# Half of each modulation block's product sums moved from VectorE to GpSimd, as one product and ten folds

## The chip, the cores and the metric

The kernel runs on one core of a Trainium2 chip. The metric is the device time of one launch in microseconds (us), from runs that each give one time; three runs of the kernel before gave 2250.38, 2250.89 and 2251.74 us. The profile names the engines PE (TensorE; PEld is its weight load), DVE (VectorE), ACT (ScalarE), POOL (GpSimd) and SP (SyncE, which here only issues DMAs).

## The reference, cut to what matters

Two transformer-like models of width 1024 over 256 tokens, one behind the other, two layers each. Before every normalisation, and behind every residual branch, vectors of 1024 scale, shift or gate the activations. These vectors come from a conditioning vector and a wide matrix:

```
s_lat = silu(c); s_ctx = silu(c_ctx)
mod   = s_lat @ w_ada[l] + b_ada[l]          # l = 0, 1: 6 * 1024 columns
mod_c = s_ctx @ w_ada[l] + b_ada[l]
...
c_act = silu(c_2)
mod   = c_act @ mod_w[layer] + mod_b[layer]  # layer = 0, 1: 9 * 1024 columns
h     = rmsnorm(x, g) * (1 + scale) + shift
x     = x + gate * branch(h)
```

With one conditioning vector (or two, in the first layer) the matrix product is a sum of 1024 products for each column of the matrix: 30720 columns in all. The rest of the work, some thirty large matrix products (feed-forward, attention, convolution branches), runs on TensorE.

## The kernel before

**Slabs.** All large weights come in slabs: 128 partitions x up to 2048 floats, loaded by SP into `raw[:, p]` in two halves, where p is 0 or 1 in turn. ScalarE rounds each half into `w_hi` (L744), VectorE makes the remainder `w_lo` (L1333), and TensorE multiplies with three products (L2206 to L2208, or L2345 and L2350 where two of them are joined). A `Stage` is a run of such slabs; a body of its loop is two slabs, p = 0 and p = 1. Every engine walks the same list of stages and orders itself by semaphores. Each engine's instructions run in the order in which they are written: what VectorE waits for holds back all that is written behind it.

**Modulation blocks.** The modulation matrices are cut into 120 blocks of 256 columns, m = 0 to 119 (`N_MOD`); 48 belong to the first model, 72 to the second. Blocks 0 to 21 (`N_PE = 22`) are done on TensorE. From block 22 on a block lies transposed: for each of the 128 partitions two rows of 1024 weights, the halves c = 0 and c = 1. `modraw[:, c]` holds one such half of one block (512 KB), and `cact` holds the activated conditioning vectors, the same in every partition. One VectorE instruction (L1370) multiplies `modraw[:, c]` by `cact` and adds up the 1024 products into one column of `modcol`; an accumulator read of 0.08 us belongs to it. Blocks 22 to 31 (below `N_BOTH = 32`) need both conditioning vectors, and so a further product with the second one, into the scratch `mod_spare` (L1367).

**Where the blocks stand.** A stage's `mods` says how its blocks are spread. With `mods=1` a body does one block, half c = 0 at slab p = 0 and half c = 1 at slab p = 1 (the up stages of the feed-forward parts, and the down stages behind them). With `mods=2` each slab does a whole block. `mods` and `mod_product` (L1342, L1357) are called in the midst of a slab's other VectorE work.

**Loads.** GpSimd issues the loads (`load_mod`, L693). There is one buffer for each half. Half c of block m is loaded when VectorE has done half c of block m - 1: the wait is for `mod_done`, which L1370 raises by one for each half. VectorE waits for `mod_in[c]` before it reads. GpSimd does nothing else from block 22 on.

**Readers of the sums.** `mod_vector` (L1407) reads 8 columns of `modcol` behind a wait for `mod_done`, at the norms and at the ends of branches, on VectorE.

Of the kernel before, what the change touches and what calls it, by code (L numbers as in the profile page):

```python
# [26 lines left out]
D = 1024  # L27
# [40 lines left out]
N_MOD_A, N_MOD_B = 6 * D // 256, 9 * D // 256  # L68
N_MOD = 2 * N_MOD_A + 2 * N_MOD_B
# [3 lines left out]
N_PE = 22  # L73
N_BOTH = N_MOD_A + 8
# [5 lines left out]
LRU_WARM = (8, 3)  # L80
SBO_EARLY = 2
ST_AHEAD = 3

F32 = mybir.dt.float32
F32R = mybir.dt.float32r
ALU = mybir.AluOpType
# [7 lines left out]
AHEAD = N_FIRST + (N_TWO - N_FIRST) // 2 - 1  # L94
# [60 lines left out]
def build(nc, a):  # L155
# [93 lines left out]
    m = N_FIRST  # L249
# [87 lines left out]
    with ExitStack() as ctx:  # L337
        def sb(name, shape, dt=F32):
            return ctx.enter_context(nc.sbuf_tensor(name, shape, dt))

        def sem(name):
            return ctx.enter_context(nc.semaphore(name))
# [65 lines left out]
        mod_spare = view(3072, 2, D)  # L408
# [110 lines left out]
        first_in = [sem(f"first_in{k}") for k in range(N_FIRST)]  # L519
        mod_in = [sem("mod_in0"), sem("mod_in1")]  # L520
        mod_next_in = [sem("mod_next_in0"), sem("mod_next_in1")]
        mod_mm, mod_row, mod_turn, mod_done = (sem(f"mod_{k}") for k in ("mm", "row", "turn", "done"))
        vec_in = [sem(f"vec_in{k}") for k in range(2)]
        c_ready, masks_in, eps_set = sem("c_ready"), sem("masks_in"), sem("eps_set")
        dve_chain, act_chain = sem("dve_chain"), sem("act_chain")
# [162 lines left out]
        @block.gpsimd  # L688
        def _(pool):
            def load_mod(m, c, freed, used):  # L690

                pool.wait_ge(freed, used)
                nc.gpsimd.dma_start(modraw[:, c, :], a["w_mod"][m, :, D * c:D * (c + 1)]).then_inc(mod_in[c], 16)  # L693

            nc.gpsimd.memset(ccol[:], 0.0).then_inc(ccol_set, 1)
            for c in range(2):

                load_mod(N_FIRST, c, first_in[N_FIRST - 1], 16)
            nc.gpsimd.dma_start(res["x"][:], a["x"]).then_inc(setup_in[3], 16)
            nc.gpsimd.dma_start(cact[:].rearrange("p v d -> p (v d)"), a["vectors"][:, 0:2 * D]).then_inc(vec_in[1], 16)  # L700
            for m in range(N_FIRST + 1, N_TWO, 2):
                for c in range(2):

                    pool.wait_ge(mod_mm, 2 * N_FIRST if m == N_FIRST + 1 else 2 * m - 3 + c)
                    nc.gpsimd.dma_start(mod_next[:, c, :], a["w_mod"][m, :, D * c:D * (c + 1)])\
                        .then_inc(mod_next_in[c], 16)
                for c in range(2):
                    load_mod(m + 1, c, mod_mm, 2 * m - 1 + c)
            with pool.Fori(N_TWO + 1, N_PE) as m:
                for c in range(2):  # L710
                    load_mod(m, c, mod_mm, 2 * m - 1 + c)
            for c in range(2):

                load_mod(N_PE, c, mod_mm, 2 * N_PE - 1 + c)
            with pool.Fori(N_PE + 1, N_BOTH + 4) as m:
                for c in range(2):
                    load_mod(m, c, mod_done, 2 * m - 1 + c)

            pool.wait_ge(mod_done, 2 * N_BOTH)
            nc.gpsimd.dma_start(cact[:, 1, :], a["vectors"][:, 2 * D:3 * D]).then_inc(vec_in[1], 16)  # L720
            with pool.Fori(N_BOTH + 4, N_MOD) as m:
                for c in range(2):
                    load_mod(m, c, mod_done, 2 * m - 1 + c)


        @block.scalar
        def _(act):
# [202 lines left out]
            def st_terms(k):  # L930

                w, zm = sb_z[:, k % 3, 0], sb_z[:, k % 3, 1]
                act.wait_ge(st_zm, k + 1)
                wait_up(act, st_o, k - 2)
                link(nc.scalar.activation(w, zm, ACT.Abs))
                link(nc.scalar.activation(w, w, ACT.Exp, scale=-1.0))
                nc.scalar.activation(w, w, ACT.Ln, bias=1.0).then_inc(st_ln, 1)

            def st_weights(k):

                act.wait_ge(st_v, k + 1)
# [374 lines left out]
        def _(dve):  # L1316
# [25 lines left out]
            def mods(s, b, p, is_first=False, last=False):  # L1342

                if last_turn(s, b, p) is not None:
                    mod_sums(last_turn(s, b, p))
                if s.m0 < N_PE:
                    if s.mods == 2:
                        mod_sums(s.m0 + 2 * b + p - 1)
                    if s.mods == 1 and p == whole(s) and not (is_first and s.m0 in NOTHING_LEFT):
                        mod_sums(s.m0 + b - 1)  # L1350
                elif s.mods == 2:
                    for c in range(2):
                        mod_product(s, s.m0 + 2 * b + p, c)
                elif s.mods == 1 and not (is_first and s.mods_from):
                    mod_product(s, s.m0 + b - s.mods_from, p)

            def mod_product(s, m, p):  # L1357


                at = m if isinstance(m, int) else s.m0  # L1360
                second_block = at >= 2 * N_MOD_A
                dve.wait_ge(c_ready, 4 if second_block else 3)
                dve.wait_ge(mod_in[p], 16 * (m - AHEAD))
                if at < N_BOTH:

                    dve.wait_ge(mod_done, 2 * m - 1 + p)
                    nc.vector.scalar_tensor_tensor(out=mod_spare[:, p, :], in0=modraw[:, p, :], scalar=1.0, in1=cact[:, 1, :],  # L1367
                                                   op0=ALU.mult, op1=ALU.mult,
                                                   accum_out=modcol[:, 1, bass.ds(2 * m + p, 1)])
                nc.vector.scalar_tensor_tensor(out=modraw[:, p, :], in0=modraw[:, p, :], scalar=1.0,  # L1370
                                               in1=cact[:, int(second_block), :], op0=ALU.mult, op1=ALU.mult,
                                               accum_out=modcol[:, 0, bass.ds(2 * m + p, 1)]).then_inc(mod_done, 1)

            def pad_edges(s):

# [31 lines left out]
            def mod_vector(r, v, out, plus, ks=range(DC), need=None):  # L1407

                if r["kind"] == "a":
                    base, bcol, w = 48 * r["l"], f"b_ada{r['l']}", 1 if r["x"] == "ctx" else 0  # L1410
                else:
                    base, bcol, w = 96 + 72 * r["l"], f"mod_b{r['l']}", 0
                k, n = ks.start, len(ks)
                dve.wait_ge(mod_done, 2 * (r["need"] if need is None else need))
                src = modcol[:, w, base + 8 * v + k:base + 8 * v + k + n]
                link(nc.vector.scalar_tensor_tensor(out=cols[:, out, k:k + n], in0=src, scalar=plus,
                                                    in1=pcol(bcol, 8 * v + k, n), op0=ALU.add, op1=ALU.add))
# [675 lines left out]
            def do_stick(n):  # L2093
                sv = next(s for what, s in plan if what == "slabs" and s.kind == "v" and s.arg["heads"] == SB_H)
                for i in range(ST_AHEAD, SB_P + 3):
                    if ST_AHEAD < i <= SB_P:
                        st_softplus(i - 1)
# [101 lines left out]
        def _(pe):  # L2199
# [850 lines left out]
```

## Time and profile before

| | |
|---|---|
| median of three runs | 2250.89 us |
| the profiled execution's own time | 2255.51 us |
| its span on the core, first to last instruction | 2253.5 us |
| PE busy | 2167.5 us (96%) |
| DVE busy | 1808.6 us (80%) |
| ACT busy | 1246.7 us (55%) |
| POOL busy | 120.4 us (5%) |
| mean granted TensorE clock | 0.986 |

The profile counts an engine as busy while an instruction runs on it; starts and durations come from one execution. Between two instructions of one engine that follow closely, the records overlap a little (a 1024-element VectorE instruction reads 1.22 us, and the next starts 1.14 us after it), so distances from start to start are the better measure in a full stretch. Idle time is put down to what ended it ("the releaser").

### The profile page before, as it was taken

What the parts mean: (1) busy time and instruction counts of PE and PEld (TensorE: products, weight loads), DVE (VectorE), ACT (ScalarE), POOL (GpSimd) and SP (SyncE); (2) the same over time, 40 slices, a digit from 0 to 9 for tenths busy, and PEclk for the clock granted to TensorE, in tenths of its full rate; (3) what the DMA queues carried; (4) which work ended last, traced back from release to release, by engine and by line L of the source; (5) the groups of instructions that cost most, each with busy time, mean ns of one, the idle gap of its engine ahead of it and who ended that gap; (6) DMA issues with size and microseconds to landing.
All of it is one profiled execution on the core that took longest, in us unless ns stands there. A gap on an engine that the chain in (4) does not pass through costs nothing.

```text
span 2253.5 us, 42557 instructions
## 1 busy us (share of the span) xinstructions
PE 2167.5 (96%) x15168; PEld 1984.7 (88%) x15168; DVE 1808.6 (80%) x3102; ACT 1246.7 (55%) x1981; POOL 120.4 (5%) x232
## 2 busy tenths in 40 slices
PE   7998999999999989999999999999999999999998
PEld 5897988888788779889999889997989989999898
DVE  4886797777677768978998988877988888889865
ACT  4466457544223333576664664656664655686653
POOL 0100000000010100000000001000010001000000
PEclk8999999999999999999999999999999999999999
DMA  9845553434475555535788688773788788636754
GB/s 360 284 132 172 182 175 127 151 130 133 137 261 184 180 178 172 178 118 166 239 271 275 227 282 266 231 245 122 246 277 272 230 280 279 232 125 192 243 177 132
DMA packets 139741, 465.59 MB, mean 207 GB/s; under 512 B 16208, under 2 KB 20432, under 8 KB 138064
## 3 DMA queue, kind: packets, MB, share of 16 engines
q1 hardware_dynamic: 102560, 339.41, 44.8%
q0 software_dynamic: 32688, 120.08, 17.1%
q10 hardware_dynamic: 4352, 4.20, 0.6%
q8 instruction: 92, 1.51, 0.3%
q14 instruction: 49, 0.40, 0.0%
HBM read 462.57 MB, written 1.05 MB: 206 GB/s over the span
## 4 chain that ended last, share of the span: by engine, by line
PE 74%; DVE 12%; ACT 6%; issue 4%; DMA 3%; ACTq 0%; SPq 0%; DVEq 0%; POOL 0%; POOLq 0%
PE bank_pair L2206 16%; PE bank_pair L2208 16%; PE bank_pair L2207 16%; PE bank_pair L2345 12%; PE bank_pair L2350 6%; DVE w_lo L1333 3%; DMA modraw<-in_w_mod 2%; DVE arena L1648 2%; ACT w_hi L744 2%; PE bank_pair L2335 2%; DVE small L1762 1%; PE ps_o L2219 1%; ACT arena L1011 1%; DVE arena L1823 1%; PE ps_o L2853 1%
## 5 line engine op out<-in xcount | busy, mean ns | idle before, releaser
L1333 DVE TENSOR_TENSOR w_lo<-raw,w_hi 128x1024 fp32r<-128x1024 f32 (+2 forms) x672 | 735.5, 1118 | 124.8 <-ACT w_hi L744 120.3
L744 ACT ACTIVATE w_hi<-raw 128x1024 fp32r<-128x1024 f32 (+2 forms) x672 | 640.5, 969 | 334.2 <-PE bank_pair L2208 193.1
L2206 PE MATMUL bank_pair<-e_both,w_hi 128*128 128x256 f32 (+1 forms) x1632 | 470.9, 289 | 11.3 <-DVE w_lo L1333 7.7
L2206 PE MATMUL bank_pair<-h_joint,w_hi 128*128 128x256 f32 (+1 forms) x1488 | 464.5, 312 | 8.1 <-DVE w_lo L1333 3.4
L2207 PE MATMUL bank_pair<-e_both,w_hi 128*128 128x256 f32 (+1 forms) x1632 | 464.1, 284 | 0.0
L2208 PE MATMUL bank_pair<-e_both,w_lo 128*128 128x256 f32 (+1 forms) x1632 | 464.0, 284 | 0.0
L2207 PE MATMUL bank_pair<-h_joint,w_hi 128*128 128x256 f32 (+1 forms) x1488 | 456.7, 307 | 0.0
L2208 PE MATMUL bank_pair<-h_joint,w_lo 128*128 128x256 f32 (+1 forms) x1488 | 456.5, 307 | 0.0
L2206 PEld LDWEIGHTS bank_pair<-e_both,w_hi 128*128 128x128 f32 x1632 | 314.9, 193 | 22.0 <-DVE w_lo L1333 9.9
L2207 PEld LDWEIGHTS bank_pair<-e_both,w_hi 128*128 128x128 f32 x1632 | 315.2, 193 | 0.3
L2208 PEld LDWEIGHTS bank_pair<-e_both,w_lo 128*128 128x128 f32 x1632 | 315.0, 193 | 0.0
L2206 PEld LDWEIGHTS bank_pair<-h_joint,w_hi 128*128 128x128 f32 x1488 | 285.4, 192 | 33.2 <-issue 14.1
L2345 PE MATMUL bank_pair<-h_joint,w_hi 128*128 128x512 f32 x1216 | 304.6, 393 | 0.1
L2207 PEld LDWEIGHTS bank_pair<-h_joint,w_hi 128*128 128x128 f32 x1488 | 285.7, 192 | 12.9
L2208 PEld LDWEIGHTS bank_pair<-h_joint,w_lo 128*128 128x128 f32 x1488 | 285.5, 192 | 12.4
L1370 DVE SCALAR_TENSOR_TENSOR modraw<-modraw,cact 128x1024 f32<-128x1024 f32 x196 | 238.1, 1220 | 32.5 <-DMA modraw<-in_w_mod 32.2
L2345 PEld LDWEIGHTS bank_pair<-h_joint,w_hi 128*128 128x128 f32 x1216 | 218.8, 189 | 39.2 <-DVE e_plain L1473 0.3
L693 POOL DMA_DIRECT2D modraw<-in_w_mod x216 | 114.1, 529 | 1954.2 <-DVE modraw L1370 1742.0
L2350 PEld LDWEIGHTS bank_pair<-h_joint,w_lo 128*128 128x128 f32 x1216 | 165.9, 191 | 11.8
L2350 PE MATMUL bank_pair<-h_joint,w_lo 128*128 128x256 f32 x1216 | 169.6, 283 | 0.0
L1648 DVE SCALAR_TENSOR_TENSOR arena<-arena,par 128x256 f32<-128x256 f32 x360 | 149.8, 479 | 4.0 <-PE bank_pair L2807 3.8
L2032 DVE SCALAR_TENSOR_TENSOR arena<-bank_pair,par,arena 128x510 f32<-128x510 f32 (+1 forms) x168 | 93.0, 621 | 47.8 <-ACT arena L1174 47.6
(258 smaller groups left out, 2636.1 us busy)
## 6 DMA issues: line engine op xcount, KB each, us to landing
modraw<-in_w_mod POOLq DMA_DIRECT2D x216, 512.0 KB, 5.2
raw<-in_w_gu SPq DMA_DIRECT2D x176, 512.0 KB, 5.5
raw<-in_w_up SPq DMA_DIRECT2D x88, 512.0 KB, 5.4
raw<-in_w_gate SPq DMA_DIRECT2D x48, 512.0 KB, 4.1
raw<-in_w_dn SPq DMA_DIRECT2D x64, 384.0 KB, 4.8
raw<-in_w_dn SPq DMA_DIRECT2D x64, 320.0 KB, 4.0
raw<-in_w_glu SPq DMA_DIRECT2D x24, 512.0 KB, 5.4
raw<-in_w_merge SPq DMA_DIRECT2D x24, 512.0 KB, 3.7
```

Source lines behind the costliest of these rows:

```text
L693: nc.gpsimd.dma_start(modraw[:, c, :], a["w_mod"][m, :, D * c:D * (c + 1)]).then_inc(mod_in[c], 16)
L744: nc.scalar.activation(w_hi[:, p, HALF * f:HALF * f + w], raw[:, p, HALF * f:HALF * f + w], ACT.Copy)\
L1333: nc.vector.tensor_tensor(w_lo[:, p, at], raw[:, p, HALF * f:HALF * f + w], w_hi[:, p, at].bitcast(F32), ALU.subtract).then_inc(lo_ready, 1)
L1370: nc.vector.scalar_tensor_tensor(out=modraw[:, p, :], in0=modraw[:, p, :], scalar=1.0, in1=cact[:, int(second_block), :], op0=ALU.mult, op ...
L1648: ins = nc.vector.scalar_tensor_tensor(out=o, in0=u, scalar=w[:, j, t:t + 1], in1=o, op0=ALU.mult, op1=ALU.add)
L2032: nc.vector.scalar_tensor_tensor(out=o, in0=i_, scalar=taps[:, c, 0:1] if left else taps[:, c, 2:3], in1=o, op0=ALU.mult, op1=ALU.add)\
L2206: nc.tensor.matmul(out, l[0], r[0], start=start, stop=False)
L2207: nc.tensor.matmul(out, l[0], r[1], start=False, stop=False)
L2208: return nc.tensor.matmul(out, l[1], r[0], start=False, stop=stop)
L2335: ins = nc.tensor.matmul(pb[p][:, f, 0:T], raw[:, p, c:c + P], h_plain[:, k, :], start=k == 0, stop=k == DC - 1)
L2345: nc.tensor.matmul(pb[p][:, f, :].rearrange("p (e t) -> p e t", e=2), w_hi[:, p, c:c + P], h_sides[:, :, k, :], start=k == 0, stop=False)
L2350: ins = nc.tensor.matmul(pb[p][:, f, T:2 * T], w_lo[:, p, c:c + P], h_hi[:, k, :], start=False, stop=k == DC - 1)
```

## The change

GpSimd takes the half c = 1 of every block from 22 on. It multiplies `modraw[:, 1]` by the vector (1024 elements) and then folds: it adds the upper half of the row to the lower half, 512 elements, then 256, and so on down to 2, and a last add of one element writes the column of `modcol`. That is 11 instructions for each product sum, each but the first behind a wait for the one ahead (`mod_step`). Blocks 22 to 31 have two product sums. The last add raises `mod_pool`.

VectorE keeps half c = 0, at p = 0 of a `mods=1` body and once per slab with `mods=2`; its instruction raises `mod_done` by two. GpSimd's queue holds the loads too: half 1 of the next block is issued behind its own last add, and half 0 behind that, once VectorE has done half 0 of the block (`next_block`). `mod_vector` waits for `mod_pool` as well.

```diff
+            def product_sum(tile, v, out, done):
+                nc.gpsimd.tensor_tensor(tile, modraw[:, 1, :], cact[:, v, :], ALU.mult).then_inc(mod_step, 1)
+                for k in range(1, FOLDS):
+                    w = D >> k
+                    pool.wait_ge(mod_step, done + k)
+                    nc.gpsimd.tensor_tensor(tile[:, 0:w], tile[:, 0:w], tile[:, w:2 * w], ALU.add).then_inc(mod_step, 1)
+                pool.wait_ge(mod_step, done + FOLDS)
+                return nc.gpsimd.tensor_tensor(out, tile[:, 0:1], tile[:, 1:2], ALU.add)
...
+            def first_vector(m, v):
+                pool.wait_ge(mod_in[1], 16 * (m - AHEAD))
+                product_sum(modraw[:, 1, :], v, modcol[:, 0, bass.ds(2 * m + 1, 1)], FOLDS * (m + N_BOTH - 2 * N_PE))                    .then_inc(mod_pool, 1)
+            def next_block(m):
+                load_mod(m, 1, mod_pool, m - N_PE)
+                load_mod(m, 0, mod_done, 2 * m)
...
-                    for c in range(2):
-                        mod_product(s, s.m0 + 2 * b + p, c)
-                elif s.mods == 1 and not (is_first and s.mods_from):
-                    mod_product(s, s.m0 + b - s.mods_from, p)
+                    mod_product(s, s.m0 + 2 * b + p)
+                elif s.mods == 1 and p == 0 and not (is_first and s.mods_from):
+                    mod_product(s, s.m0 + b - s.mods_from)
...
-                dve.wait_ge(mod_done, 2 * (r["need"] if need is None else need))
+                blocks = r["need"] if need is None else need
+                dve.wait_ge(mod_done, 2 * blocks)
+                if blocks > N_PE:
+                    dve.wait_ge(mod_pool, blocks - N_PE)
```

GpSimd, the loop over blocks with one vector: before.

```order
L693 ISA [waits mod_done]
L693 DMA modraw<-in_w_mod 128x1024
L693 ISA [waits mod_done]
L693 DMA modraw<-in_w_mod 128x1024
L721 REGISTER_ALU
L721 COMPARE_AND_BRANCH
```

The same loop after the change, down to the third fold; seven more instructions of the same kind follow, ending in one element.

```order
L694 ISA [waits mod_pool]
L694 DMA modraw<-in_w_mod 128x1024
L693 REGISTER_ALU
L694 REGISTER_ALU [waits mod_done]
L694 DMA modraw<-in_w_mod 128x1024
L734 ISA
L718 TENSOR_TENSOR modraw<-modraw,cact 128x1024 [waits mod_in1]
L721 ISA
L722 TENSOR_TENSOR modraw<-modraw 128x512 [waits mod_step]
L721 REGISTER_ALU
L722 TENSOR_TENSOR modraw<-modraw 128x256 [waits mod_step]
L721 REGISTER_ALU
```

The two loads stood in the queue alone; the product and the folds now stand between one pair of loads and the next.

VectorE, from the middle of an up body of the second model's feed-forward (L1333 makes the low part of a half slab, L2053, L2066 and L2075 belong to the gated activation): before.

```order
L1333 TENSOR_TENSOR w_lo<-raw,w_hi 128x1024 [waits hi_ready]
L2053 ISA [waits upb_hi]
L2053 TENSOR_TENSOR e_both<-arena,e_both 128x256
L2066 TENSOR_TENSOR arena<-bank_pair,arena 128x512 [waits upb_side]
L1370 ISA [waits mod_in1,c_ready]
L1370 SCALAR_TENSOR_TENSOR modraw,modcol<-modraw,cact 128x1024
L2069 REGISTER_ALU
L2075 TENSOR_TENSOR arena<-arena 128x256 [waits upb_silu]
```

The same place after the change (L1369, L2091, L2104 and L2113 are the same lines of the new file).

```order
L1369 TENSOR_TENSOR w_lo<-raw,w_hi 128x1024 [waits hi_ready]
L2091 ISA [waits upb_hi]
L2091 TENSOR_TENSOR e_both<-arena,e_both 128x256
L2104 TENSOR_TENSOR arena<-bank_pair,arena 128x512 [waits upb_side]
L2107 REGISTER_ALU
L2113 TENSOR_TENSOR arena<-arena 128x256 [waits upb_silu]
```

The product at p = 1 and its wait for the load are gone; the one at p = 0, with its wait for `mod_in0`, stands where it stood.

## Rows read from the trace of the kernel before

**Rows 1.** The page: busy time and share of the span by engine.
```profile
PE 2167.5 (96%) x15168; PEld 1984.7 (88%) x15168; DVE 1808.6 (80%) x3102; ACT 1246.7 (55%) x1981; POOL 120.4 (5%) x232
```
**Rows 2.** Stretches with blocks: length, busy us (instructions) by engine, clock, DMA share, GB/s.
```profile
core 0: us, PE busy (x) PEld busy (x) DVE busy (x) ACT busy (x) POOL busy (x), PEclk, DMA share, GB/s
520.00:570.00 50.00, 50.00 (x222) 41.41 (x221) 38.09 (x55) 20.40 (x29) 2.64 (x5) 1.00 0.43 140
620.00:650.00 30.00, 30.00 (x134) 24.87 (x133) 21.83 (x36) 6.58 (x7) 4.23 (x8) 1.00 0.72 246
1085.00:1186.00 101.00, 101.00 (x844) 101.00 (x843) 101.00 (x181) 64.36 (x106) 9.52 (x18) 1.00 0.82 271
1310.00:1383.00 73.00, 73.00 (x432) 64.78 (x431) 62.05 (x93) 42.44 (x66) 7.39 (x14) 1.00 0.84 274
1386.00:1419.00 33.00, 33.00 (x277) 33.00 (x277) 30.50 (x50) 11.48 (x16) 4.22 (x8) 1.00 0.89 290
```
**Rows 3.** Waits of PE, whole span: for whom, us in total, times, longest.
```profile
PE bank_pair L2206 <- DVE w_lo L1333: 14.0, 12, 2.7
PE bank_pair L2206 <- DVE arena L2032: 11.9, 3, 4.9
```
**Rows 4.** Groups by line and form: count, busy us, mean ns, idle before and its releaser.
```profile
L1333 DVE TENSOR_TENSOR w_lo<-raw,w_hi 128x1024 fp32r<-128x1024 f32 x464 | 555.3, 1222 | 94.6 <-ACT w_hi L744 92.4
L1370 DVE SCALAR_TENSOR_TENSOR modraw<-modraw,cact 128x1024 f32<-128x1024 f32 x196 | 238.1, 1220 | 32.5 <-DMA modraw<-in_w_mod 32.2
L1367 DVE SCALAR_TENSOR_TENSOR arena<-modraw,cact 128x1024 f32<-128x1024 f32 x20 | 24.4, 1220 | 4.2 <-issue 4.2
```
**Rows 5.** The load line L693 on GpSimd: durations, and time from issue to landing.
```profile
L693 POOL DMA_DIRECT2D modraw<-in_w_mod x216: 527/527/662, 33.0 to 2105.4; - x108
DMA to landing us min/median/max: 3.7/5.2/9.9
```
**Rows 6.** GpSimd in an up stretch: start us, us, what, idle before and its releaser.
```profile
1315.26 0.53 POOL L693 DMA_DIRECT2D modraw<-in_w_mod  x1 [4.00 <-DVE modraw L1370]
1320.84 0.53 POOL L693 DMA_DIRECT2D modraw<-in_w_mod  x1 [5.05 <-DVE modraw L1370]
1326.42 0.53 POOL L693 DMA_DIRECT2D modraw<-in_w_mod  x1 [5.05 <-DVE modraw L1370]
```
**Rows 7.** GpSimd in down stretches, and (668.95) behind a body with both halves together.
```profile
617.86 0.53 POOL L693 DMA_DIRECT2D modraw<-in_w_mod  x1 [4.29 <-DVE modraw L1370]
626.37 0.53 POOL L693 DMA_DIRECT2D modraw<-in_w_mod  x1 [4.29 <-DVE modraw L1370]
668.95 0.53 POOL L693 DMA_DIRECT2D modraw<-in_w_mod  x1 [0.61 <-DVE modraw L1370]
1389.12 0.53 POOL L693 DMA_DIRECT2D modraw<-in_w_mod  x1 [6.31 <-DVE modraw L1370]
1396.97 0.53 POOL L693 DMA_DIRECT2D modraw<-in_w_mod  x1 [3.54 <-DVE modraw L1370]
```
**Rows 8.** GpSimd's only computing instructions: start us, us, what.
```profile
0.49 0.10 POOL L3043 MEMSET const-uint8-127<- 128x1 uint8 x1
0.88 0.31 POOL L695 MEMSET ccol<- 128x256 f32 x1 [0.29 <-POOLq L3043]
```
**Rows 9.** VectorE in one slab of an up stretch, in order of time.
```profile
1313.38 1.22 DVE L1370 SCALAR_TENSOR_TENSOR modraw<-modraw,cact 128x1024 f32<-128x1024 f32 x1
1315.02 2.36 DVE L1333 TENSOR_TENSOR w_lo<-raw,w_hi 128x1024 fp32r<-128x1024 f32 x2
1318.36 0.69 DVE L2066 TENSOR_TENSOR arena<-bank_pair,arena 128x512 f32<-128x512 f32 x1 [0.65 <-ACT arena L1211]
```
**Rows 10.** Stretches of 4 us about a pause of TensorE (columns as in rows 2).
```profile
578.00:582.00 4.00, 0.55 (x3) 0.13 (x1) 1.93 (x3) 1.96 (x3) 0.00 (x0) 0.84 0.69 278
582.00:586.00 4.00, 2.51 (x6) 2.06 (x7) 4.00 (x8) 0.63 (x1) 0.00 (x0) 0.50 0.00 0
586.00:590.00 4.00, 4.00 (x16) 3.19 (x15) 2.18 (x5) 1.56 (x3) 0.53 (x1) 0.81 0.38 132
```

More of the change, by code:

```diff
@@ L82 @@
 ST_AHEAD = 3
+FOLDS = 10
 F32 = mybir.dt.float32
@@ L521, in build @@
         mod_next_in = [sem("mod_next_in0"), sem("mod_next_in1")]
-        mod_mm, mod_row, mod_turn, mod_done = (sem(f"mod_{k}") for k in ("mm", "row", "turn", "done"))
+        mod_mm, mod_row, mod_turn, mod_done, mod_pool, mod_step = (sem(f"mod_{k}") for k in ("mm", "row", "turn", "done", "pool", "step"))
         vec_in = [sem(f"vec_in{k}") for k in range(2)]
@@ L714, in _ @@
                 load_mod(N_PE, c, mod_mm, 2 * N_PE - 1 + c)
-            with pool.Fori(N_PE + 1, N_BOTH + 4) as m:
-                for c in range(2):
-                    load_mod(m, c, mod_done, 2 * m - 1 + c)
-            pool.wait_ge(mod_done, 2 * N_BOTH)
-            nc.gpsimd.dma_start(cact[:, 1, :], a["vectors"][:, 2 * D:3 * D]).then_inc(vec_in[1], 16)
-            with pool.Fori(N_BOTH + 4, N_MOD) as m:
-                for c in range(2):
-                    load_mod(m, c, mod_done, 2 * m - 1 + c)
+            def product_sum(tile, v, out, done):
[6 more added lines that the diff above has]
+                return nc.gpsimd.tensor_tensor(out, tile[:, 0:1], tile[:, 1:2], ALU.add)
@@ new lines, in both_vectors @@
+            def both_vectors(m):
+                pool.wait_ge(mod_in[1], 16 * (m - AHEAD))
+                product_sum(mod_spare[:, 1, :], 1, modcol[:, 1, bass.ds(2 * m + 1, 1)], 2 * FOLDS * (m - N_PE))
+                product_sum(modraw[:, 1, :], 0, modcol[:, 0, bass.ds(2 * m + 1, 1)], 2 * FOLDS * (m - N_PE) + FOLDS)                    .then_inc(mod_pool, 1)
+            def first_vector(m, v):
+                pool.wait_ge(mod_in[1], 16 * (m - AHEAD))
+                product_sum(modraw[:, 1, :], v, modcol[:, 0, bass.ds(2 * m + 1, 1)], FOLDS * (m + N_BOTH - 2 * N_PE))                    .then_inc(mod_pool, 1)
@@ new lines, in next_block @@
+            def next_block(m):
+                load_mod(m, 1, mod_pool, m - N_PE)
+                load_mod(m, 0, mod_done, 2 * m)
+            pool.wait_ge(c_ready, 3)
+            pool.wait_ge(mod_done, 2 * N_PE + 2)
+            both_vectors(N_PE)
+            with pool.Fori(N_PE + 1, N_BOTH) as m:
+                next_block(m)
+                both_vectors(m)
+            next_block(N_BOTH)
+            nc.gpsimd.dma_start(cact[:, 1, :], a["vectors"][:, 2 * D:3 * D]).then_inc(vec_in[1], 16)
@@ L726, in _ @@
+            first_vector(N_BOTH, 0)
+            with pool.Fori(N_BOTH + 1, 2 * N_MOD_A) as m:
+                next_block(m)
+                first_vector(m, 0)
+            next_block(2 * N_MOD_A)
+            pool.wait_ge(c_ready, 4)
+            first_vector(2 * N_MOD_A, 1)
+            with pool.Fori(2 * N_MOD_A + 1, N_MOD) as m:
+                next_block(m)
+                first_vector(m, 1)
         @block.scalar
@@ L1351, in mods, with mod_product @@
                 elif s.mods == 2:
-                    for c in range(2):
-                        mod_product(s, s.m0 + 2 * b + p, c)
-                elif s.mods == 1 and not (is_first and s.mods_from):
-                    mod_product(s, s.m0 + b - s.mods_from, p)
-            def mod_product(s, m, p):
+                    mod_product(s, s.m0 + 2 * b + p)
+                elif s.mods == 1 and p == 0 and not (is_first and s.mods_from):
+                    mod_product(s, s.m0 + b - s.mods_from)
+            def mod_product(s, m):
                 at = m if isinstance(m, int) else s.m0
@@ L1362, in mod_product @@
                 dve.wait_ge(c_ready, 4 if second_block else 3)
-                dve.wait_ge(mod_in[p], 16 * (m - AHEAD))
+                dve.wait_ge(mod_in[0], 16 * (m - AHEAD))
                 if at < N_BOTH:
-                    dve.wait_ge(mod_done, 2 * m - 1 + p)
-                    nc.vector.scalar_tensor_tensor(out=mod_spare[:, p, :], in0=modraw[:, p, :], scalar=1.0, in1=cact[:, 1, :],
+                    dve.wait_ge(mod_done, 2 * m)
+                    nc.vector.scalar_tensor_tensor(out=mod_spare[:, 0, :], in0=modraw[:, 0, :], scalar=1.0, in1=cact[:, 1, :],
                                                    op0=ALU.mult, op1=ALU.mult,
-                                                   accum_out=modcol[:, 1, bass.ds(2 * m + p, 1)])
-                nc.vector.scalar_tensor_tensor(out=modraw[:, p, :], in0=modraw[:, p, :], scalar=1.0,
+                                                   accum_out=modcol[:, 1, bass.ds(2 * m, 1)])
+                nc.vector.scalar_tensor_tensor(out=modraw[:, 0, :], in0=modraw[:, 0, :], scalar=1.0,
                                                in1=cact[:, int(second_block), :], op0=ALU.mult, op1=ALU.mult,
-                                               accum_out=modcol[:, 0, bass.ds(2 * m + p, 1)]).then_inc(mod_done, 1)
+                                               accum_out=modcol[:, 0, bass.ds(2 * m, 1)]).then_inc(mod_done, 2)
             def pad_edges(s):
```

## The prediction

> **What bounds the kernel now.** I read the page first. TensorE is busy 96% of the span, VectorE 80%, GpSimd 5% [rows 1]. The reader is to see that the engine that gets lighter is not the one that sets the time. The view by stretches then shows where blocks are worked: in all five TensorE is busy from end to end at full clock, while VectorE is at 73 to 100% and GpSimd at 5 to 14% [rows 2]. In the waits of TensorE the largest for VectorE are 14.0 and 11.9 us over the whole span [rows 3]; that is what a lighter VectorE can give back, at most some 20 us of 2253.5. Third I read GpSimd's own queue, since the change fills it. In an up stretch a load is issued every 5.58 us, two to a block, so a block takes 11.16 us [rows 6]; in down stretches 7.85 to 8.5 us [rows 7]. GpSimd sleeps between loads because VectorE has not freed the buffer, and the load lands 5.2 us after its issue [rows 5]. Each block so carries one landing in a period set by TensorE, with VectorE's product beside it.
>
> **What goes from VectorE.** Blocks 22 to 119 are 98; each loses one L1370, and the ten blocks 22 to 31 one L1367 as well: 108 instructions of 1.22 us [rows 4], 132 us, and with 0.08 us for each accumulator read 140 us. In the up stretch 13 instructions in 73 us leave 7; VectorE falls from 62.05 to about 54 us of 73 [rows 2]. As TensorE has no idle time in these stretches, I cost this gain at nothing. It is worth at most about 20 us, by rows 3. The stretch 1085 to 1186, where VectorE too is busy throughout [rows 2], gains no time either, since TensorE is full there as well.
>
> **What GpSimd gets.** 108 product sums of 11 instructions. The trace has no two-input instruction on GpSimd, so a sum's length C is bounded. It handles 1024 elements in the product and 1023 in the folds, 2047 in all. The fast end is VectorE's pace: 1.14 us from start to start for 1024 elements (two together last 2.36, one alone 1.22 [rows 4, 9]), 1.11 ns each, 2.3 us. The slow end takes GpSimd's own row: 256 elements written in 0.31 us against 0.10 for one [rows 8], 0.82 ns each; two reads and a write one after the other are 2.5 ns, 5.0 us. I take 4.2 us, nearer to GpSimd's row because it is the same engine. Then there is the fixed part, 11 times: between 0.10 us (the shortest instruction [rows 8]) and 0.61 us (GpSimd woken by a semaphore, with its register work, until the next load starts [rows 7]). I take 0.25, since the folds wait for GpSimd itself and carry one register operation: 2.75 us. Undisturbed, C is 7.0 us, between 3.4 and 11.7.
>
> Last comes what VectorE and GpSimd do to each other. No row shows them computing at once. The lower bound is zero; the upper is each of 11 steps standing behind one `w_lo` of 1.14 us, 12.5 us. VectorE would be busy half the time in a stretched block, its instructions are 0.4 to 1.2 us long, so I take 0.2 us a step, 2 us. **C = 9 us.**
>
> The Trainium skill has prices for both. GPSIMD Engine Reference, section 3.1, gives 4497 ns for an add of 2048 elements against VectorE's 2293; an estimate from it is 4.5 us for the 2047 elements, and C without disturbance would be 7.3, the sum below about 170 us; no row here shows a GpSimd add.
>
> **What waits for it.** This is the step that carries the forecast. GpSimd's queue now reads: load half 1 of block m, load half 0 of block m, product and folds of block m. Half 1 can only be loaded when its buffer has been folded, and half 0 is issued behind that. So the shortest period of a block is one landing plus one sum: 5.2 + C = 14.2 us. VectorE waits for half 0 in the midst of a body; behind the wait stand that body's gated activation and the next slab's `w_lo`, then TensorE. A period over the spacing of before is thus lost in full, block after block.
>
> From the issue times of L693 I took the spacing of all blocks. Of those from 32 on, 55 stand in up-like places at 11.0 us in the mean (for instance rows 6) and 23 in down stretches at 8.0 (rows 7; 8 issues, 4 blocks, in 33 us [rows 2]). Eight follow a pause of over 30 us.
> - Up: 55 x (14.2 - 11.0) = 176 us.
> - Down: 23 x (14.2 - 8.0) = 143 us.
> - Two vectors, period 5.2 + 18 = 23.2 us: blocks 23 to 27 come every 21.7 us (one slab takes about 10.8: 50 us hold five loads [rows 2]), 5 x 1.5 = 8 us; four of blocks 28 to 31 every 7.9 us, 4 x 15.3 = 61 us.
> - At each of the eight pauses GpSimd gets ahead by a load and a sum. Stepping through the 97 blocks (VectorE's time is the later of its old spacing and the last sum's end + 0.53 + 5.2 + 1.3; a sum ends C after its load has landed) gives 321 us for the whole, so the pauses give back about 67.
>
> The same stepping gives 12 us at C = 3.4, 34 at 5, 51 at 5.6, 145 at 7, 413 at 10, 597 at 12 and 781 at 14. Below about 5 it is nearly free, above 6 each further us costs some 70 to 90.
>
> **Edits at nothing.** The first sums follow VectorE's first product, block 22, with 17 us to the next: hidden. The new wait in `mod_vector` asks for blocks that lie eight or more back at the norms; it would cost up to one C at the few ends of branches if it did not. The load of the third vector, once, is 0.53 us. The two loads cost 0.53 us each [rows 5], which the queue held before too. TensorE's pauses can lower its clock: after a pause of some 5 us the granted clock is 0.50, the 1.2 GHz level, and about 6 us later it is rising again [rows 10]. In a down block TensorE would pause 6 us and then run some us at half pace, 8 us of work becoming about 11. The period of 14.2 hides this; with C below 7 it would show, at up to 3 us x 23.
>
> **The sum.** 2255.5 (the profiled execution) + 321 = 2576 us. The median of the three runs is 4.6 us below that execution, so the forecast is 2572 us.
>
> **Rivals.**
>
> A. *GpSimd runs undisturbed.* C = 7 and the period 12.2. Up 55 x 1.2, down 23 x 4.2, two vectors 40, pauses less: 145 us, 2396 us. For it speaks that the two engines work on different rows of memory; nothing shows against it.
>
> B. *The two engines shut each other out.* Each fold that finds VectorE reading waits for its end, and VectorE's `w_lo` waits for the 1024-element product. After a landing both start at once, GpSimd's 11 steps and VectorE's backlog of about 8 instructions, so nearly each step waits some 0.5 us: C = 7 + 5.5 = 12.5, about +640 us, 2890 us. For it: VectorE is at 85 to 92% in the down and up stretches [rows 2]. Against it: no row. The Trainium skill has this as a rule (SBUF — State Buffer, Who interferes with whom): a VectorE instruction with two SBUF inputs and a GpSimd instruction that reads SBUF exclude each other for the whole instruction. `w_lo` and L1370 are of that kind. No run so far shows it.
>
> C. *Short folds.* If small instructions cost about 0.1 us and elements about VectorE's pace to half as slow again, C is 3.5 to 5 and the period 8.7 to 10.2: up stretches stay whole, down stretches lose 1 to 2 us a block. That is +12 to +34 us, about 2275.
>
> D. *Faster.* The same C below 4, and VectorE's 140 us shorten the stretches that follow it: the waits of rows 3 shrink by half and the waits of VectorE for modulation loads, 32.5 us [rows 4], in part. That gives up to -15 us, 2236. It decides at C = 4, where the period, 9.2 us, exceeds the down spacing by little. Against it speaks GpSimd's 0.61 us to wake: at that price the fixed part alone is 6.7 us.
>
> **How the numbers follow.** The forecast, C from 7.5 to 11.5, has 0.42. A has 0.22, B 0.15, C 0.11, D with the cases near zero 0.10. Slower by over 0.2% (4.5 us, about what a measurement can tell from no change): 0.42 + 0.22 + 0.15 + 0.08 of C, 0.87; within 0.2%: 0.05; faster: 0.08. The range runs from 2280 (C about 4.5 to 5) to 2840 (C = 12): it leaves out D and part of C below, about 0.12, and most of B's upper part, about 0.08.
>
> **What the profile of after would show.** The load of half 1 issued right behind the last one-element add, and a distance from one such load to the next of 14 us in up and down stretches alike, where 11.2 and 8 stood. VectorE's largest new wait would be its product's, for the load of half 0. TensorE busy would fall to about 75 to 80% in rows like rows 2, with clock below 1.00 in down stretches. A GpSimd sum is read from start to start: 9 us. In rival A it is 7 with `w_lo` still at 1.22 us; in B `w_lo` has a longer mean and the folds' starts fall on the ends of VectorE's instructions; in C and D the up stretches keep 11.2 us. The forecast is wrong if GpSimd still idles before its loads in the up stretches, waiting for VectorE.

## The result, and the profile after

The changed kernel takes 2773.4 us (median of four runs, 2766.5 to 2775.4) against 2250.6 us before: 1.231 times as long, 95% interval 1.230 to 1.233. The profiled execution took 2766.5 us, its span is 2764.8 us. So the change costs 523 us (511 between the two profiled executions), where the prediction had 321. The measured time lies in its range (2280 to 2840), near the upper end.

The page of the changed kernel, its part on busy time and its chain of work that ended last (its first line answers [rows 1]); below it the same chain in the kernel before.

```profile
PE 2323.9 (84%) x15168; PEld 2093.9 (76%) x15168; DVE 1932.1 (70%) x2886; ACT 1241.2 (45%) x1981; POOL 1123.5 (41%) x1420
...
POOL 32%; PE 22%; issue 20%; DVE 15%; ACT 5%; DMA 4%; POOLq 2%; DVEq 0%; ACTq 0%; SPq 0%
```
```profile
PE 74%; DVE 12%; ACT 6%; issue 4%; DMA 3%; ACTq 0%; SPq 0%; DVEq 0%; POOL 0%; POOLq 0%
```

TensorE fell from 96 to 84% of the span. VectorE has 216 records fewer (108 products and their accumulator reads), yet its busy time rose, from 1808.6 to 1932.1 us: it lost 140 us of work and took on some 260 us by which its other instructions got longer. GpSimd, which was 5% busy and 0% of the chain, now heads the chain with 32%. VectorE's `w_lo` of 1024 elements, at 1222 ns before [rows 4]:

```profile
L1369 DVE TENSOR_TENSOR w_lo<-raw,w_hi 128x1024 fp32r<-128x1024 f32 x464 | 626.5, 1374 | 118.2 <-ACT w_hi L780 117.7
```

GpSimd's queue in an up stretch, in order of time (start us, us, what, idle before and its releaser); this answers [rows 6].

```profile
1606.20 1.19 POOL L694 DMA_DIRECT2D modraw<-in_w_mod  x2 [0.66 <-POOL modcol L724]
1610.50 2.40 POOL L718 TENSOR_TENSOR modraw<-modraw,cact 128x1024 f32<-128x1024 f32 x1 [3.11 <-DMA modraw<-in_w_mod]
1612.97 7.22 POOL L722 TENSOR_TENSOR modraw<-modraw 128x512 f32<-128x512 f32 x9
1620.37 0.19 POOL L724 TENSOR_TENSOR modcol<-modraw 128x1 f32 x1 [0.18 <-POOL modraw L722]
1621.38 1.20 POOL L694 DMA_DIRECT2D modraw<-in_w_mod  x2 [0.82 <-POOL modcol L724]
```

This is the cycle of the prediction. The one-element add ends at 1620.56; 0.82 us later both loads of the next block are issued. From load to load it is 15.18 us, where 11.16 us stood before. A sum, from the start of its product to the end of its last add, takes 10.06 us here; over all 108 sums the mean is 10.1, over those of blocks with one vector 10.2. Over the 80 distances between blocks with one vector that hold no pause the mean is 16.3 us, up and down stretches alike; the ten with two vectors are 24.1 us apart.

Who waits in the changed kernel: waits of VectorE, then of TensorE (us in total, times, longest); the second answers [rows 3].

```profile
DVE modraw L1405 <- DMA modraw<-in_w_mod: 412.8, 70, 15.3
...
PE bank_pair L2244 <- DVE w_lo L1369: 221.9, 61, 11.8
PE bank_pair L2388 <- DVE w_lo L1369: 54.6, 20, 5.6
```

VectorE's product (now L1405) waits 412.8 us for the load of half 0; it was 32.5 us [rows 4]. That load stands behind the sum in GpSimd's queue, so the releaser that the row names is the DMA, and the cause stands one step behind it. TensorE waits behind VectorE for `w_lo`.

Three stretches with blocks, columns as in [rows 2]: an up, a down and a last down stretch.

```profile
1595.00:1687.00 92.00, 72.88 (x380) 61.55 (x379) 61.70 (x76) 36.16 (x58) 61.96 (x78) 0.91 0.55 189
1687.00:1753.00 66.00, 47.65 (x333) 46.64 (x333) 42.29 (x56) 16.76 (x25) 43.68 (x52) 0.85 0.55 174
2098.00:2160.00 62.00, 43.21 (x281) 42.39 (x280) 32.91 (x39) 13.48 (x19) 43.22 (x52) 0.81 0.52 167
```

TensorE is busy 70 to 79% of them, and the granted clock fell to 0.81 to 0.91 from 1.00. No engine is full. That is what a loop of waits looks like: a landing, a sum, and an issue, one behind the other.

### The profile page after: what moved, and what is told of

Its sections match the earlier page's. It is cut to its first block, busy times and chain, and to the rows that moved or that the text cites. A ratio compares the mean times of both kernels' runs of the same rounds, so it can differ in the third digit from the quotient of the medians.

```text
span 2764.8 us, 44709 instructions
## 1 busy us (share of the span) xinstructions
PE 2323.9 (84%) x15168; PEld 2093.9 (76%) x15168; DVE 1932.1 (70%) x2886; ACT 1241.2 (45%) x1981; POOL 1123.5 (41%) x1420
## 4 chain that ended last, share of the span: by engine, by line
POOL 32%; PE 22%; issue 20%; DVE 15%; ACT 5%; DMA 4%; POOLq 2%; DVEq 0%; ACTq 0%; SPq 0%
POOL modraw L722 19%; POOL modraw L718 7%; PE bank_pair L2244 5%; PE bank_pair L2245 5%; PE bank_pair L2246 5%; DVE w_lo L1369 4%; POOL arena L722 3%; DVE arena L1686 2%; DMA modraw<-in_w_mod 2%; POOL modraw L694 2%; ACT w_hi L780 2%; PE bank_pair L2383 2%; POOLq L721 1%; POOL arena L718 1%; PE bank_pair L2388 1%
## 5 line engine op out<-in xcount | busy, mean ns | idle before, releaser
L1369 DVE TENSOR_TENSOR w_lo<-raw,w_hi 128x1024 fp32r<-128x1024 f32 (+2 forms) x672 | 852.0, 1291 | 139.9 <-ACT w_hi L780 138.2
L722 POOL TENSOR_TENSOR modraw<-modraw 128x512 f32<-128x512 f32 (+8 forms) x882 | 628.6, 713 | 69.1
L2244 PE MATMUL bank_pair<-e_both,w_hi 128*128 128x256 f32 (+1 forms) x1632 | 493.2, 302 | 103.2 <-DVE w_lo L1369 97.6
L2244 PE MATMUL bank_pair<-h_joint,w_hi 128*128 128x256 f32 (+1 forms) x1488 | 478.7, 322 | 79.5 <-DVE w_lo L1369 71.9
L2245 PE MATMUL bank_pair<-e_both,w_hi 128*128 128x256 f32 (+1 forms) x1632 | 482.0, 295 | 0.0
L2245 PE MATMUL bank_pair<-h_joint,w_hi 128*128 128x256 f32 (+1 forms) x1488 | 466.4, 313 | 0.0
L1405 DVE SCALAR_TENSOR_TENSOR modraw<-modraw,cact 128x1024 f32<-128x1024 f32 x98 | 174.9, 1785 | 413.1 <-DMA modraw<-in_w_mod 412.8
L2244 PEld LDWEIGHTS bank_pair<-e_both,w_hi 128*128 128x128 f32 x1632 | 334.2, 205 | 119.2 <-DVE w_lo L1369 104.3
L2244 PEld LDWEIGHTS bank_pair<-h_joint,w_hi 128*128 128x128 f32 x1488 | 293.2, 197 | 113.3 <-DVE w_lo L1369 80.2
L718 POOL TENSOR_TENSOR modraw<-modraw,cact 128x1024 f32<-128x1024 f32 x98 | 237.9, 2427 | 314.8 <-DMA modraw<-in_w_mod 314.6
L2383 PE MATMUL bank_pair<-h_joint,w_hi 128*128 128x512 f32 x1216 | 331.7, 418 | 20.8 <-DVE arena L2104 20.8
L2245 PEld LDWEIGHTS bank_pair<-e_both,w_hi 128*128 128x128 f32 x1632 | 334.6, 205 | 0.5
L2246 PEld LDWEIGHTS bank_pair<-e_both,w_lo 128*128 128x128 f32 x1632 | 333.6, 204 | 0.0
L2245 PEld LDWEIGHTS bank_pair<-h_joint,w_hi 128*128 128x128 f32 x1488 | 294.3, 198 | 13.9
L2383 PEld LDWEIGHTS bank_pair<-h_joint,w_hi 128*128 128x128 f32 x1216 | 235.3, 203 | 70.8 <-issue 23.0
```

What stands on the lines that cost most here:

```text
L718: nc.gpsimd.tensor_tensor(tile, modraw[:, 1, :], cact[:, v, :], ALU.mult).then_inc(mod_step, 1)
L722: nc.gpsimd.tensor_tensor(tile[:, 0:w], tile[:, 0:w], tile[:, w:2 * w], ALU.add).then_inc(mod_step, 1)
L1369: nc.vector.tensor_tensor(w_lo[:, p, at], raw[:, p, HALF * f:HALF * f + w], w_hi[:, p, at].bitcast(F32), ALU.subtract).then_inc(lo_ready, 1)
L1405: nc.vector.scalar_tensor_tensor(out=modraw[:, 0, :], in0=modraw[:, 0, :], scalar=1.0, in1=cact[:, int(second_block), :], op0=ALU.mult, op ...
L2244: nc.tensor.matmul(out, l[0], r[0], start=start, stop=False)
L2245: nc.tensor.matmul(out, l[0], r[1], start=False, stop=False)
```

## The experiments

Each experiment ran beside the kernel before on the same chip, which gave 2251.1 us; that is the "before" of this section. Two theories stood against each other. *Queue*: the loss is the order, a period of one landing and one sum, with VectorE's load standing behind the sum. *Port*: the loss is that reads by GpSimd and reads by VectorE exclude each other.

### What taking the products off VectorE is worth: e4_no_half1

```diff
-                nc.gpsimd.tensor_tensor(tile, modraw[:, 1, :], cact[:, v, :], ALU.mult).then_inc(mod_step, 1)
-                for k in range(1, FOLDS):
...
-                return nc.gpsimd.tensor_tensor(out, tile[:, 0:1], tile[:, 1:2], ALU.add)
+                return nc.gpsimd.tensor_tensor(out, modraw[:, 1, 0:1], modraw[:, 1, 1:2], ALU.add)
```

> The sums of the halves c = 1 are left out on all engines but for one add of one element on GpSimd; the loads stay. It gives what taking 108 products (140 us of its time) off VectorE is worth if nothing is paid for it. Theory 'TensorE sets the time before': 0 to 20 us under before, 2230 to 2250 us. Rival 'VectorE was the bound in stretches such as 1085 to 1186 us, where it is busy throughout': 30 us or more under before.

Measured: 2247.1 us, ratio 0.998 (0.9975 to 0.9994): 4 us under before. The gain that the change aims at was never there. VectorE's 140 us were covered by TensorE, also in the stretch where VectorE was busy throughout. About the same stretch in this kernel, columns as in [rows 2]:

```profile
1080.00:1180.00 100.00, 100.00 (x836) 100.00 (x835) 91.35 (x162) 64.67 (x106) 19.09 (x26) 1.00 0.79 277
```

VectorE has 8.65 us of idle time in 100 us; TensorE is as full as before. The rival, that VectorE set the time there, would have given 30 us or more, and falls.

One thing about the kernels that follow: in e1, e6, e7 and e10 GpSimd's loop over blocks is written out, while the changed kernel, e2, e3, e4 and e8 keep it. From the last add of a sum to the issue of the next load it is 0.76 us (mean of 79) in the changed kernel, with register work and a branch between, and 0.31 us in e1 and e6.

### Writes in the place of reads: e1_writes_only

```diff
+W0 = 1024
...
-                nc.gpsimd.tensor_tensor(tile, modraw[:, 1, :], cact[:, v, :], ALU.mult).then_inc(mod_step, 1)
-                for k in range(1, FOLDS):
...
-                    nc.gpsimd.tensor_tensor(tile[:, 0:w], tile[:, 0:w], tile[:, w:2 * w], ALU.add).then_inc(mod_step, 1)
+                for k in range(FOLDS):
...
+                    nc.gpsimd.memset(tile[:, 0:W0], 0.0).then_inc(mod_step, 1)
```

> The product and the ten folds on GpSimd are replaced by ten instructions that only write (1024 elements each, 0.82 ns per element by the memset row, about 0.94 us each), each still behind a wait for the one ahead, then the last add; so the length of a sum stays about 10 us but GpSimd reads almost nothing. The sums of the halves c = 1 are left out. The loop over blocks is written out. Theory 'queue' (period = landing + sum, VectorE waits for the load that stands behind the sum in GpSimd's queue): period stays 15 to 16 us, time 2650 to 2770 us, though w_lo is back at 1.22 us. Theory 'port' (the time is lost because reads of GpSimd and VectorE exclude each other): time falls to 2250 to 2320 us.

Measured: 2737.2 us (ratio 1.217, 1.214 to 1.219). Its groups by form (count, busy us, mean ns, idle before and its releaser), as in [rows 4]:

```profile
L1369 DVE TENSOR_TENSOR w_lo<-raw,w_hi 128x1024 fp32r<-128x1024 f32 x464 | 554.4, 1219 | 117.0 <-ACT w_hi L780 116.4
L1405 DVE SCALAR_TENSOR_TENSOR modraw<-modraw,cact 128x1024 f32<-128x1024 f32 x98 | 119.9, 1224 | 553.8 <-DMA modraw<-in_w_mod 553.5
...
L722 POOL MEMSET modraw<- 128x1024 f32 x980 | 934.1, 953 | 383.0 <-DMA modraw<-in_w_mod 332.3
```

`w_lo` is at 1219 ns, as before [rows 4], and the time is still 486 us over before. So the queue alone, with sums of this length, makes a loss of this size; VectorE need not be slowed at all. But the sum's length is a free quantity here, since I set it near that of the changed kernel (10.5 us in the mean, against 10.2). What makes the changed kernel's sum that long is the next question.

### The length of an undisturbed sum: e6_writes_7us

The shortest records of the eleven instructions in the changed kernel (512 elements, for example, range from 1278 to 2272 ns in a sample of 36) are 2332, 1278, 733, 453, 317, 250, 219, 202, 202, 193 and 192 ns: 6.4 us, and with ten gaps of about 0.09 us 7.3 us. The shortest of the changed kernel's 108 sums, as a whole, is 7.31 us, so this length does occur. This kernel, an edit of e1, was to write for that long; its sums have a mean of 7.0 us.

```diff
-W0 = 1024
+W0 = 606
```

> As e1_writes_only, with 606 instead of 1024 elements in each of the ten writing instructions, so that a sum lasts 7.3 us, the sum of the shortest durations of the changed kernel's eleven instructions. It stands for the change on a chip where GpSimd's reads disturb nobody. The sums of the halves c = 1 are left out. Theory 'queue, and collisions of reads lengthen the sum': by the stepping with C = 7.3, 171 us over before, 2405 to 2440 us; the rest of the 522 us, some 340, then belongs to reads. Rival 'a sum's own length makes the whole loss': it would have to stay above 2650 us.

Measured: 2463.1 us (ratio 1.094, 1.092 to 1.096), 212 us over before; the stepping had 171, and the time lies above the range that was expected. From its queue, in order of time:

```profile
1412.61 6.59 POOL L722 MEMSET modraw<- 128x606 f32 x10 [4.78 <-DMA modraw<-in_w_mod]
1419.28 1.09 POOL L724 TENSOR_TENSOR modcol<-modraw 128x1 f32<-128x1 f32 x1
1420.67 1.10 POOL L695 DMA_DIRECT2D modraw<-in_w_mod  x2 [0.30 <-POOL modcol L724]
1427.32 6.59 POOL L722 MEMSET modraw<- 128x606 f32 x10 [5.56 <-DMA modraw<-in_w_mod]
```

From the issue at 1420.67 to the next start it is 6.65 us; the mean over 79 blocks with one vector is 5.75 us, and from the end of one sum to the start of the next 6.1 us, where the stepping has 5.2 (with 5.9 it gives 225). So the longer way from sum to sum can account for the missing 41 us.

The comparison splits the loss: 212 us are there without the reads, the other 310 only with them. Nearly all of the 310 lies in the distance between blocks, 13.2 us in the mean here and 16.3 in the changed kernel, and that is the sum's length, 7.0 against 10.2; the way from sum to sum is about equal (6.1 and 5.9 us), since e6's quicker issue and its longer landing cancel. One small share of the 310 is not the reads' own: e6's sums are 0.3 us shorter than an undisturbed one, worth some 20 us by the 78 us for each us of sum between e6 and e1 (274 us for 3.5 us). So the reads are worth rather 290 us.

### The order of the queue: e2_two_buffers

```diff
+        mod_more = sb("mod_more", [P, D])
...
-                load_mod(m, 1, mod_pool, m - N_PE)
-                load_mod(m, 0, mod_done, 2 * m)
...
+            def one(k, odd, work, *v):
+                load1(k + odd, 1 - odd)
+                work(k, odd, *v)
+                next0(k + odd, 1 - odd)
```

Odd blocks have their half 1 in `mod_more`. `load1` loads half 1 of the next block into the other buffer, `work` is the block's product and folds, and `next0` loads half 0 of the next block.

> Half 1 gets a second buffer; its next load is issued ahead of the sum instead of behind it. Same sums, same order of folds. Theory 'queue': the period becomes one sum and two issues, about 11.5 us; up stretches (11.2 us before) lose next to nothing, down stretches 3.5 us a block, the two-vector blocks in the down stretch some 50 us together: 2350 to 2420 us. Theory 'port': as many reads collide in less time, so the time stays near 2770, at least above 2650 us.

Measured: 2489.5 us (ratio 1.107, 1.105 to 1.109). The queue's order is worth 284 us, which *port* alone cannot explain. But the time is 70 us above the range that I had given to *queue*, so the order is not all. Its period in a down stretch:

```profile
1411.57 3.05 POOL L720 TENSOR_TENSOR mod_more<-mod_more,cact 128x1024 f32<-128x1024 f32 x1
1414.70 7.50 POOL L724 TENSOR_TENSOR mod_more<-mod_more 128x512 f32<-128x512 f32 x9
...
1424.63 2.41 POOL L720 TENSOR_TENSOR modraw<-modraw,cact 128x1024 f32<-128x1024 f32 x1
```

From product to product it is 13.06 us: a sum of 11.8 us and two issues, and no waiting for a landing. (Over all blocks with one vector the mean distance is 12.8 us.) In the stretch from 1500 to 1560 us (columns as in [rows 2]) both engines that share the reads are nearly full, and TensorE is not:

```profile
1500.00:1560.00 60.00, 51.46 (x338) 47.74 (x339) 54.60 (x63) 25.64 (x39) 52.31 (x62) 0.94 0.67 215
```

### Two buffers and no reads: e7_two_buffers_writes

The edit is that of e6_writes_7us, made in e2_two_buffers, and GpSimd's loop is written out.

> e2_two_buffers with the writing instructions of e6_writes_7us in the place of the sums (7.3 us, the sums of the halves c = 1 left out). The stepping with two buffers and C = 7.3 gives 36 us over before: 2275 to 2300 us. If e2's 239 us came from its queue order or from load traffic and not from reads, it would stay near 2450 us or more.

Measured: 2270.3 us (ratio 1.008, 1.006 to 1.011), 19 us over before; the stepping had 36, and the range began at 2275. The landing hidden and the reads gone, nearly the whole loss is gone. Of e2's 239 us, 219 go with the reads and the loop. The loop's part is small but not separated: between sums e2 takes 1.20 or 1.70 us by turns, the branch in every second one, where e7 takes 1.03 at the shortest; 0.4 us for each of 80 to 90 distances would be some 35 us.

### One instruction that reads, or two that write: e3_product_only, e10_short_writes

```diff
-FOLDS = 10
+FOLDS = 1
...
                 nc.gpsimd.tensor_tensor(tile, modraw[:, 1, :], cact[:, v, :], ALU.mult).then_inc(mod_step, 1)
-                for k in range(1, FOLDS):
-                    w = D >> k
-                    pool.wait_ge(mod_step, done + k)
-                    nc.gpsimd.tensor_tensor(tile[:, 0:w], tile[:, 0:w], tile[:, w:2 * w], ALU.add).then_inc(mod_step, 1)
```

> The folds are left out (the sums of the halves c = 1 are left out): GpSimd makes the product of 1024 elements and the last add of one, a sum of about 2.9 us. Theory 'queue': by the stepping of the prediction 5 to 15 us over before, 2255 to 2270 us. Theory 'port': GpSimd's reading time falls from 9.2 to 2.7 us a sum, so about 0.29 of the 522 us remain: about 2400 us.

```diff
-FOLDS = 10
+FOLDS = 2
+W0 = 1024
...
-                nc.gpsimd.tensor_tensor(tile, modraw[:, 1, :], cact[:, v, :], ALU.mult).then_inc(mod_step, 1)
...
+                for k in range(FOLDS):
...
+                    nc.gpsimd.memset(tile[:, 0:W0], 0.0).then_inc(mod_step, 1)
```

> As e3_product_only, with two writing instructions of 1024 elements (0.95 us each) in the place of the product: a sum of about 2.4 us that reads next to nothing. The sums of the halves c = 1 are left out. Theory 'e3's 52 us are collisions of reads': the time is that of e4_no_half1, 2245 to 2255 us. Rival 'they come from the loads being issued behind the product': it stays at 2285 to 2305 us.

Measured: 2303.0 us for the product alone (ratio 1.022, 1.020 to 1.025) and 2246.2 us with writes (0.998, 0.997 to 0.999). With a sum this short the queue costs nothing, looped or written out, so e10 sits beside e4, and the 57 us between e3 and e10 go with the reads: 0.53 us for each of 108 products. `w_lo` of 1024 elements has a mean of 1467 ns in e3 and 1220 ns in e10; the first row is of e3_product_only, the second of e10_short_writes.

```profile
L1365 DVE TENSOR_TENSOR w_lo<-raw,w_hi 128x1024 fp32r<-128x1024 f32 x464 | 669.6, 1467 | 113.1 <-ACT w_hi L776 112.4
```
```profile
L1369 DVE TENSOR_TENSOR w_lo<-raw,w_hi 128x1024 fp32r<-128x1024 f32 x464 | 555.2, 1220 | 118.2 <-ACT w_hi L780 117.7
```

Both theories missed e3: *queue* had 15 us at most, since its stepping has no term for a slower VectorE, and *port*, scaled by reading time, had about 150.

### The blocks with two vectors: e8_one_sum_each

```diff
-                product_sum(mod_spare[:, 1, :], 1, modcol[:, 1, bass.ds(2 * m + 1, 1)], 2 * FOLDS * (m - N_PE))
+                nc.gpsimd.tensor_tensor(modcol[:, 1, bass.ds(2 * m + 1, 1)], cact[:, 0, 0:1], cact[:, 1, 0:1], ALU.mult)
```

> The changed kernel without GpSimd's sum for the second vector in blocks 22 to 31 (that sum is left out). The stepping with C = 10.2 gives 431 us with two sums and 352 with one: 79 us less, so about 2695 us. If two sums in a block were hidden, since six of the ten blocks stand 21 us apart, it would be within 30 us of the changed kernel.

Measured: 2707.1 us (ratio 1.203, 1.198 to 1.207), 66 us under the changed kernel, against 79 expected. The edit also lowers the counts that the waits for `mod_step` ask for. The second sum of these ten blocks is not hidden.

### What the runs add up to

| | reads as in the change | writes only |
|---|---|---|
| load behind the sum | 2773.4 (+523) | 2463.1 (+212), sum of 7.0 us |
| load ahead of the sum | 2489.5 (+239) | 2270.3 (+19), sum of 7.1 us |
| product only | 2303.0 (+52) | 2246.2 (-5) |

The columns differ by 310, 219 and 57 us; of the first some 20 are the shorter sum, of the second a part is the loop, and the rest goes with the reads. The two causes strengthen each other, since 212 and 239 are 451 and the change costs 523: a collision makes the sum longer, and the queue charges each longer sum to every block. None of these kernels is faster than the kernel before by more than 5 us, and e4, which leaves the work out, puts what VectorE's relief is worth at 4.

## How the reads collide

The timeline of VectorE and GpSimd in the changed kernel over 4.6 us, from narrow windows (start us, us, what):

```profile
1612.50 1.48 DVE L1405 SCALAR_TENSOR_TENSOR modraw<-modraw,cact 128x1024 f32<-128x1024 f32 x1 [3.07 <-DMA modraw<-in_w_mod]
1612.97 2.16 POOL L722 TENSOR_TENSOR modraw<-modraw 128x512 f32<-128x512 f32 x1
...
1613.91 1.50 DVE L2113 TENSOR_TENSOR arena<-arena 128x256 f32<-128x256 f32 x1
1615.21 0.80 POOL L722 TENSOR_TENSOR modraw<-modraw 128x256 f32<-128x256 f32 x1
...
1615.34 1.76 DVE L1369 TENSOR_TENSOR w_lo<-raw,w_hi 128x1024 fp32r<-128x1024 f32 x1
1616.09 1.32 POOL L722 TENSOR_TENSOR modraw<-modraw 128x128 f32<-128x128 f32 x1
```

The records begin when an instruction is started, also if it cannot yet read. GpSimd's product ended at 1612.90; VectorE's product, started at 1612.50, ended at 1613.98, 1.08 us after that. GpSimd's fold of 512 elements had started at 1612.97, and ended at 1615.13, 1.15 us after VectorE's end, where the shortest such fold takes 1.26. VectorE's 256-element instruction, which takes 0.42 us before, started at 1613.91 and ended at 1615.41, 0.28 us after the fold. GpSimd's next fold ended at 1616.01, 0.60 us after that, and `w_lo` at 1617.10, 1.09 us later. Each instruction does its own work only when the other engine's has ended: they take strict turns. L1405, L2113 and `w_lo` all have two inputs in SBUF.

This is no matter of one place. Wherever in the changed kernel the record of one of these three overlaps with that of one of GpSimd's products or folds, the one that ends later ends behind the other by its own shortest duration, less at most 0.15 us: a `w_lo` of 1024 elements by at least 1.07 us (133 such pairs; alone it takes 1.20 at the shortest), a VectorE product by at least 1.08 us (80; 1.21), a fold of 512 elements by at least 1.11 us (118; 1.26), one of 128 by at least 0.30 us (85; 0.45). In e1, where GpSimd only writes, a `w_lo` ends as little as 0.003 us behind a write. L2104 has its first input in PSUM (where TensorE leaves its results) and only its second in SBUF: 37 of its 80 runs overlap with GpSimd's product or folds, and these take 676 to 682 ns, against a mean of 691 before.

The Trainium skill says this (SBUF — State Buffer, Who interferes with whom): the second SBUF input of a VectorE instruction comes through the read interface that GpSimd uses, and the later of the two blocks until the earlier has finished. These traces agree with that rule, in the turns of 1612 to 1617 us, in the writes and in the PSUM input.

## Why the prediction was right, and where it was off

**No gain from VectorE.** Right: costed at nothing, bounded by 20 us, measured 4 us (e4).

**The period is a landing and a sum.** Right, and it carried the forecast: the load of half 1 behind the last add, equal periods in up and down stretches, VectorE's new wait at half 0, all as named beforehand. e1 shows that this mechanism alone makes a loss of 486 us with sums of 10.5 us (ten records of 0.953, gaps of 0.06 and the last add), where the stepping gives 459. Hiding the landing takes 284 of the 523 us away with reads (e2), and 193 of the 212 without (e7).

**An undisturbed sum of 7.0 us.** Right in sum: 7.3 by the shortest records, and 7.31 for the shortest whole sum. Of that, elements cost 2.1 ns (2332 - 192 ns over 1023), so 4.3 us against 4.2, and the fixed part is about 0.27 us with its gap against 0.25.

**0.2 us a step for collisions.** This is the term that was too small. C was 10.1 us, not 9: collisions cost 2.8 us a sum, 0.26 a step. In the stepping that is 101 us of the missing 200 (422 at C = 10.1 against 321).

**5.2 us between two sums.** The second mis-sized term. Over 79 distances of blocks with one vector, 5.9 us lie between the end of one sum and the start of the next: 5.17 us from the issue to the next product, as forecast, and 0.76 us that GpSimd takes from its last add to the issue, which I had left out. With 5.9 us in the place of 5.2 the stepping gives 479 at C = 10.1, and with the 10.2 us of blocks with one vector some 490.

**What remains.** Some 35 us. The comparison with e1 tells where they lie. The 90 distances between blocks that hold no pause add up to the same in both profiled executions, 1545 us in the changed kernel and 1547 in e1, while the seven pauses between stretches of blocks last 603 us against 576: that is the 27 us between the two. So VectorE's longer instructions add no more than some 30 us to what the cycle of waits takes, and they do it in and around the pauses. The mean of its product rose from 1.22 to 1.79 us, but that does not lengthen the cycle: there the product runs beside GpSimd's longer sum. In e3 the product is at 1.24 us and `w_lo` at 1.47, so the 57 us there go with `w_lo` and say nothing of the product. What lengthens the pauses was not traced.

**The number.** The time lies in the range because the range reached to C = 12. The sum itself was short by 202 us, 321 against 523, and both terms named here were too small, so that nothing made up for them.

**The rivals.** B, that the two engines shut each other out, had the mechanism right and its size too large: its C was 12.5 us and its time 2890 us. I had written that no row speaks for it; the runs now do. Its error and mine are the same term, the price of a collision: 2 us in mine, 5.5 in B, 2.8 measured. I had also given A the higher chance. One sign named for B was off: it is the folds' ends, not their starts, that are set by VectorE's instructions. A, that GpSimd runs undisturbed, falls. e6 is what it would have been: its sum is 7.0 us as in A, but its time is 2463 us and not 2396, with 6.1 us from one sum to the next in the place of 5.2. That the two engines work on different halves of `modraw` did not keep them apart. C, short folds, and D, a faster kernel, fall by the 7.3 us.

**The clock.** I costed TensorE's pauses at nothing, hidden by the period. The clock did fall, to 0.81 in a down stretch, and TensorE was only 70% busy there. That speaks for the cover; no run shows what the clock alone costs here.

## What to carry to other kernels

Before work is moved to an idle engine, look at what its queue already carries: here the new work was put between a load and the next, in a ring with one buffer, and the period became the load's landing plus the work. Price GpSimd's elementwise work by instruction (about 0.27 us fixed and 2.1 ns an element in these traces, so that the ten folds cost twice what the one product of 1024 elements does), and add that each instruction that reads SBUF takes turns with VectorE's instructions of two SBUF inputs. Ask first what the relieved engine is worth with the work simply left out: that one run gave 4 us.

## What was not expected of the hardware

The alternation is strict down to short instructions: a fold of 128 elements, 0.45 us at its shortest, took 1.32 us behind a `w_lo`. A record's duration, where the two engines overlap, then does not tell the engine's own speed; the difference between the end of the other engine's instruction and its own end does. A GpSimd instruction that only writes (953 ns for 1024 elements) leaves VectorE untouched, at the same engine load.
